# RWKV pairs: three kinds of places lose their dense passes, which go to other runs of the same pair

## The reference, cut to what matters

```
z = h + shift_mu * (h_prev - h)                     # h = x_normed @ w_in, columns of r, k, v and low-rank inputs
w_log = -softplus(-(w0 + tanh(wd) @ w2)) - 0.5      # low-rank product
a = sigmoid(a0 + ad @ a2)                           # low-rank product
g = sigmoid(gd) @ g2                                # low-rank product
def step(S, inp):                                   # per head, token after token
    Sa = einsum('bhvk,bhk->bhv', S, a_t)
    S = S * w_t + Sa * b_t + v_t * k_t
    return S, einsum('bhvk,bhk->bhv', S, r_t)
y = ((y - mean(y)) * rsqrt(var(y) + eps)) * lnx_g + lnx_b
y = (y + bonus) * g
```

## Time and profile before

| | |
|---|---|
| median of 3 runs | 2621.03 us (2619.11 to 2621.68) |
| the profiled execution | 2618.16 us |
| its span in the profile | 2616.3 us |
| TensorE busy in the span | 2570.2 us (98%) |
| VectorE, ScalarE, GpSimd busy | 1399.3, 684.6 and 1507.3 us |
| granted TensorE clock, mean | 0.997 |

### The profile page before, as it was taken

How to read it: one execution, slowest core, us unless ns; L and a number is a source line. 1 busy time by engine, 2 the same in 40 slices (tenths; PEclk the granted TensorE clock), 3 DMA queues, 4 the chain that set the end, 5 groups by cost and what they waited for, 6 DMA issues and landing times.

```text
span 2616.3 us, 47481 instructions
## 1 busy us (share of the span) xinstructions
PE 2570.2 (98%) x16344; PEld 2016.0 (77%) x16344; DVE 1399.3 (53%) x1989; ACT 684.6 (26%) x1274; POOL 1507.3 (58%) x963
## 2 busy tenths in 40 slices
PE   8989999998999999999999999999999999999999
PEld 6768888876777778788888887777778788888887
DVE  7866555455556647663443434466647663433434
ACT  3452000024134436521100002134436521100002
POOL 5666666655545454556666666545454556666664
PEclk9999999999999999999999999999999999999999
DMA  4213323323211122223233233311132223233332
GB/s 163 69 45 112 96 92 93 97 76 114 81 50 51 51 91 68 73 85 100 89 96 93 92 96 111 92 47 51 50 94 65 73 85 100 90 95 96 89 96 97
DMA packets 72446, 222.61 MB, mean 85 GB/s; under 512 B 9313, under 2 KB 12257, under 8 KB 72289
## 3 DMA queue, kind: packets, MB, share of 16 engines
q1 hardware_dynamic: 72000, 220.46, 27.3%
q10 hardware_dynamic: 288, 0.04, 0.0%
HBM read 218.37 MB, written 2.10 MB: 84 GB/s over the span
## 4 chain that ended last, share of the span: by engine, by line
PE 93%; DVE 2%; issue 1%; DMA 1%; POOL 1%; DVEq 1%; ACT 0%; SPq 0%; ACTq 0%; POOLq 0%
PE acc L537 81%; PE bank L537 10%; POOL w_lo L367 1%; DMA raw<-in_w_pg 1%; PE bank L1142 0%; DVE y_lo L1180 0%; DMA raw<-in_w_in 0%; POOL w_hi L360 0%; DMA x<-in_x 0%; SPq L319 0%; DVE att L1389 0%; DVEq L1625 0%; DVEq L1390 0%; DVE rw_kp L1649 0%; PE bank L1101 0%
## 5 line engine op out<-in xcount | busy, mean ns | idle before, releaser
L367 POOL TENSOR_TENSOR w_lo<-raw,w_hi 128x1024 fp32r<-128x1024 f32 (+3 forms) x438 | 963.1, 2199 | 326.2 <-PE acc L537 270.5
L360 POOL TENSOR_SCALAR w_hi<-raw 128x1024 fp32r<-128x1024 f32 (+3 forms) x438 | 431.7, 986 | 635.1 <-PE acc L537 532.7
L537 PE MATMUL acc<-xg_hi,w_hi 128*128 128x512 f32 x2208 | 593.9, 403 | 11.8 <-issue 4.7
L537 PE MATMUL acc<-xg_lo,w_hi 128*128 128x512 f32 x2208 | 581.8, 399 | 0.0
L537 PE MATMUL acc<-xg_hi,w_lo 128*128 128x512 f32 x2208 | 577.5, 398 | 0.0
L537 PEld LDWEIGHTS acc<-xg_hi,w_hi 128*128 128x128 f32 x2208 | 409.2, 188 | 123.0 <-issue 28.6
L537 PEld LDWEIGHTS acc<-xg_lo,w_hi 128*128 128x128 f32 x2208 | 412.6, 189 | 99.5 <-issue 1.5
L537 PEld LDWEIGHTS acc<-xg_hi,w_lo 128*128 128x128 f32 x2208 | 411.7, 188 | 100.6 <-issue 1.9
L2045 ACT ACTIVATE ffn_act<-ffn_t 128x512 f32<-128x512 f32 x100 | 63.3, 633 | 770.9 <-DVEq L1240 619.5
L1180 DVE TENSOR_TENSOR x<-x,acc 128x512 f32<-128x512 f32 x104 | 71.4, 687 | 320.3 <-PE acc L537 319.8
L537 PE MATMUL acc<-hid_hi,w_hi 128*128 128x512 f32 x656 | 182.7, 396 | 3.1 <-POOL w_lo L367 1.6
(11 more groups left out here) (346 smaller groups left out, 2753.7 us busy)
## 6 DMA issues: line engine op xcount, KB each, us to landing
raw<-in_w_up SPq DMA_DIRECT2D x132, 512.0 KB, 3.6
raw<-in_w_down SPq DMA_DIRECT2D x48, 512.0 KB, 3.6
raw<-in_w_gate SPq DMA_DIRECT2D x48, 512.0 KB, 3.6
raw<-in_w_ret SPq DMA_DIRECT2D x32, 512.0 KB, 3.6
raw<-in_w_rw SPq DMA_DIRECT2D x28, 512.0 KB, 3.7
raw<-in_w_o SPq DMA_DIRECT2D x48, 256.0 KB, 2.6
raw<-in_w_in SPq DMA_DIRECT2D x18, 512.0 KB, 3.7
raw<-in_w_down SPq DMA_DIRECT2D x24, 384.0 KB, 3.0
```

The lines of the kernel that those rows point to most:

```text
L360: nc.gpsimd.tensor_scalar(w_hi[:, s, 0:n], raw[:, s, 0:n], 1.0, 0.0, ALU.mult, ALU.add).then_inc(w_half[s], 1)
L367: nc.gpsimd.tensor_tensor(w_lo[:, s, 0:n], raw[:, s, 0:n], bits(w_hi[:, s, 0:n]), ALU.subtract).then_inc(w_split[s], 1)
L537: return nc.tensor.matmul(o, a, b, start=first, stop=last, skip_group_check=shared)
```

## The change

Only the table changes, and the rule that picks its row. The sum of every row stays at 96, so all passes are still issued, in the same order, in the same pair. What changes is how many stand at each place.

```
-                FILLS = ((22, 4, 4, 5, 5, 4, 5, 3, 5, 4, 5, 5, 3, 4, 2, 2, 2, 3, 3, 3, 3),
-                         (7, 3, 4, 6, 6, 5, 6, 4, 6, 1, 6, 7, 7, 5, 3, 2, 2, 4, 4, 4, 4))
+                FILLS = ((23, 4, 4, 6, 5, 5, 5, 0, 6, 4, 6, 6, 4, 4, 0, 0, 0, 3, 3, 4, 4),
+                         (10, 3, 4, 7, 6, 6, 6, 0, 7, 0, 7, 7, 8, 5, 0, 0, 0, 5, 5, 5, 5),
+                         (7, 3, 4, 7, 6, 5, 6, 4, 6, 0, 6, 7, 7, 5, 3, 2, 2, 4, 4, 4, 4))
...
-                    fills = iter(FILLS[min(j, 1)])
+                    fills = iter(FILLS[(j + 1) // 2])
```

## The result

The changed kernel takes 2635.31 us (median of 5 runs, 2633.15 to 2637.87), the kernel before 2621.68 us (5 runs on the same chip, 2619.11 to 2623.36). The ratio is 1.0053, with an interval of 1.0039 to 1.0067. The loss is 13.6 us, where 7.5 us were forecast: the direction was right, the size was not, and the time lies above the range.

A forecast was written before the change was run, and what follows sets the result against it. TensorE was taken to bound the kernel (93% of the chain). Losses of 3.2, 1.2, 2.1 and 1.0 us summed to 7.5 us, giving a median of 2628.5 us, 0.29% slower; range 2624.8 to 2631.5 us.

The forecast's parts named there:

- pairs 1 and 2 (places 7, 14, 15, 16): Passes leave low-rank products, sums and state steps in both layers; losses of 3.2, 1.2 and 2.1 us.
- pair 0, twice: Nine passes arrive, three into idle time; 1.17 + 0.05 us paid, 0.32 and 0.41 us back: 0.49 us lost, twice.
- pair 3, twice: One pass goes from place 9 to place 3: zero.
- at places 10, 11 and 12 TensorE is idle for 0.43, 0.88 and 0.58 us, so three are free: Pair 0: three of nine arriving passes cost nothing; those idle times, called VectorE's, shrink by 0.23 us each.
- idle time at places whose passes I call covered: One of the signs, looked for in the changed trace, that would show the prediction wrong; no size given.
- more than the sum: Rival, chance 0.08: a further wait, on weights not yet split, or idle pieces in six pairs; 3.9 us more, 2632.4 us.
- The term of place 14: Sums, pairs 1 and 2, both layers: three passes leave, start 0.18 us behind VectorE's additions; 0.35 and 0.24 us lost, 1.2 us.
- place 7: Low-rank products, pairs 1 and 2: four passes leave, ScalarE's copy into `rw_AW` won't come sooner; 0.79 us per pair, 3.2 us.
- places 15 and 16: State steps, pairs 1 and 2: four passes leave, third step starts 0.41 us earlier; 0.53 us lost per pair, 2.1 us.
- place 9: Variance, pairs 1, 2 and 3: one pass leaves and comes back elsewhere; zero, up to 1.1 us won in six places.
- the sums of pair 0: Place 14 of pair 0: sums start at 775.18 instead of 775.50, 0.18 us behind the small block's last product; 0.32 us back.

The follow-up runs named there:

- acc_early: Changed kernel, table untouched; in pair 0 VectorE scales the second slot out of its accumulator at level 4 instead of 5: 2627.27 us, single run (before: 2622.79).
- qev_last: Changed kernel with TensorE's waits ahead of the sums reordered to `y0`, `kks`, then `qev` last: 2636.99 us, single run.
- p0_cap72: Changed kernel with two passes of pair 0 moved from place 11 to 12, so 72 stand ahead of level 5 `rw_G,rw_Y`: 2632.57 us, ratio 1.0038.
- only14: Kernel before, but in pairs 1 and 2 the three passes of place 14 stand at places 17 to 19: 2626.97 us, single run (before: 2623.20).
- only7: Kernel before, but in pairs 1 and 2 the four passes of place 7 stand at place 8: 2622.05 us, single run (before: 2623.20).
- only15_16: Kernel before, but in pairs 1 and 2 the four passes of places 15 and 16 stand at 17 to 20: 2620.61 us, single run (before: 2623.20).
- p0_only: Kernel before with only pair 0's row of the table changed: 2627.57 us, ratio 1.0018.

## Why the prediction was wrong

Forecast and measured, in us, from the stretches of both layers:

| term | forecast | measured |
|---|---|---|
| pairs 1 and 2 (places 7, 14, 15, 16) | 6.5 | 7.65 |
| pair 0, twice | 1.0 | 6.6 |
| pair 3, twice | 0 | 0.3 |
| sum | 7.5 | 14.6 |

(Pair 1: 50.89 - 48.95 and 50.89 - 48.91. Pair 2: 1.23 and 1.10, each with the 0.70 us of its own place 0 added. Pair 0: 4.06 and 3.96, each less 0.70; its own place 0, ahead of the stretch, cost nothing: the 12.80 us from the sums ahead of it to its first product stayed.) The two regions have 14.6 us. The timed loss of 13.6 us and the span's 15.0 us lie on either side.

**The step that failed** is the one on pair 0: "at places 10, 11 and 12 TensorE is idle for 0.43, 0.88 and 0.58 us, so three are free". I took the idle time at 11 as belonging to whatever stands there. But passes are not alike: the 73rd starts a slot, and has a wait of its own. I never counted the passes ahead of each place against the slots' boundaries, though the table alone gives that count. From `rw_X,rw_TL` of level 5 to `rw_SCB,rw_AU` there were 771.12 - 763.87 = 7.25 us, and now there are 774.71 - 764.98 = 9.73 us: 2.48 us where I had none, 5.0 us in the two layers.

The same piece in the other runs takes this apart. With the accumulator free it is 7.27 us (acc_early); with the wait, but at full clock, 8.70 us (first layer of qev_last); with the wait and the lower clock 9.73 us. So the wait is worth 1.4 us and the clock 1.0 us more. The clock stretched the work by 1.45 us (0.44 in `rw_G,rw_Y`, 1.13 - 0.69; 0.87 in the four passes, 2.07 - 1.20; 0.14 in `rw_AW,rw_G`, 1.24 - 1.10), but part of that fell where TensorE would have been idle ahead of `rw_AW,rw_G` (0.35 us in acc_early). Without the crossing (p0_cap72) the same piece is 7.43 us, 2.3 us less.

What I had called a sign of being wrong, idle time at places whose passes I call covered, is what came. The rival "more than the sum" had a pass that reaches its slot too early, but blamed the split weights, and its price was taken from another place; the resource was the accumulator. The other 1.6 us of pair 0's 6.6 (1.19 and 0.39 us in acc_early) are nearer to the 1.0 forecast.

**The term of place 14 was mis-sized**: 1.2 us, where 7.65 - 3.1 - 2.2 = 2.4 us are left for it. I took 0.18 us from VectorE's end to TensorE's start, a row in which TensorE had one wait. In pair 1 three waits stand in a row and the first is the late one, which makes 0.48 us, as it did before under the passes, so nearly the whole 0.70 us is lost (only14: 0.71 and 0.74). qev_last shows the 0.3 us. In pair 2 the sums did come 0.37 and 0.25 us nearer to the end of the small product, but the idle piece without a releaser ahead of it grew (0.19 to 0.45 and 0.30 to 0.34 us). That part has no cause that a run shows.

**Right were** place 7 (3.2 forecast, 4 x 0.78 = 3.1 measured; only7 has 0.77 and 0.78 where 0.79 was forecast), places 15 and 16 (2.1; 4 x 0.54 = 2.2) and place 9, as far as it shows: it was not tried alone, and pair 3, which changes only there and at place 3, lost 0.31 and 0.02 us. That is no more than it differs by where its row is unchanged: from its first product to the last product of g it took 56.54 to 57.13 us in only7, only14, only15_16 and p0_only, and 56.91 and 56.90 us in the changed kernel. The Trainium skill, "TensorE: Matmul & The Clock Gate", section "Wait — 56ns, not 53.3ns?", has 215.7 ns from start to start of products with 512 columns at full clock; an estimate by it has place 7 losing 4 x 0.2157 - 0.15 = 0.71 us a pair, and the runs show 0.77 and 0.78. At the sums of pair 0 I had 0.32 us to win and 0.04 us were lost (771.12 to 775.50 before, 774.71 to 779.13 after): the sums start 0.39 us behind the product and not 0.18, so 0.11 us came back, and an idle piece of 0.75 instead of 0.65 us took nearly all of it.

**What stays open**: the pieces of idle time without a releaser inside `rw_SCK,rw_tokV`. In pair 0 they were 0.55 to 1.24 us in the kernels here, in pair 2 0.19 to 1.00 us, and changed with edits far from them. No run tells their cause. They make up to 0.6 us per pair between kernels. Why the clock fell in five cases of the same wait and not in the sixth is open too.

## What to carry to other kernels

Idle time ahead of an instruction is free only to work that has no wait of its own that ends later: before moving work into it, count where the moved work crosses into another buffer, and find on the other engine what frees that buffer. Work that is moved away from a place uncovers everything that stood behind it, so read how many waits stand there in a row, and put the late one last; which one that is can differ from place to place, and the same order won time in pair 1 and lost some in pair 0. And a single idle time of TensorE can cost more than the wait itself, since the clock may fall behind it: 1.4 us and 1.0 us more here.

## What the runs showed of the hardware

**The clock.** Behind an idle time of 1.86 to 1.90 us TensorE's granted clock fell to 0.50, its lower level of 1.2 GHz, for some 3 us, in five of six cases (both layers of the changed kernel and of p0_only, the second layer of qev_last), and not in the sixth. From `rw_X,rw_TL` of level 5 to `rw_SCB,rw_AU` TensorE took 9.73 to 9.81 us in the five cases and 8.70 us in the sixth, so the fall cost 1.0 to 1.1 us. Behind the 0.88 us of before and the 1.10 us of p0_cap72 it stayed at 1.00. The Trainium skill, "TensorE: Matmul & The Clock Gate", section "What's actually happening", says that the clock is halved or full by how busy TensorE was of late; the two levels are what these rows show.

**Waits in a row.** Two waits behind a late one cost TensorE 0.3 us (0.49 against 0.17 us from VectorE's end to the sums), and a second one behind a late one 0.16 us (0.55 against 0.39 us from the end of its own product to the sums).

**A stretched VectorE instruction.** The TENSOR_SCALAR of pair 0 took 1.80 us in the changed kernel and 1.30 us in acc_early, where it started 0.49 us later; its end stayed at 1.86 and 1.85 us behind the start of `rw_X,rw_TL`. So its length is not its own work alone. In GpSimd's timeline of the two kernels, the changed one first, an instruction beside it ends at 766.55 and 765.27 us, and VectorE's ends 0.29 and 0.28 us later:

```profile
764.17 2.38 POOL L367 TENSOR_TENSOR w_lo<-raw,w_hi 128x1024 fp32r<-128x1024 f32 x1 [6.34 <-DVEq L1626]
```

```profile
762.89 2.38 POOL L367 TENSOR_TENSOR w_lo<-raw,w_hi 128x1024 fp32r<-128x1024 f32 x1 [6.34 <-DVEq L1626]
```

That it waits for GpSimd fits both, but no run moves the one without the other, so this stays a reading.
